# A transformer layer's down projection: seven products of half blocks in place of a direct product

## The chip, the cores and the metric
One core of a Trainium2 chip runs the whole kernel. The metric is the device time of one execution in microseconds (us). The kernel before takes 816.16 us, the median of three runs (816.03 to 816.21).

## The reference
One layer of a streaming encoder over 576 tokens (512 of a prompt, 64 of a sample), width 1024, all float32: normed input projection, two groups of attention heads, an output projection, cross-attention into a memory, and then the part that matters here:

```
hf = rms_norm(x, g_ffn)
x = x + (silu(hf @ w_gate) * (hf @ w_up)) @ w_down      # w_gate, w_up: 1024 x 2816, w_down: 2816 x 1024
y = rms_norm(x, g_final)
```

## The kernel before
Five engines run five hand-written queues, tied together by semaphores. Activations lie transposed in SBUF: 128 features on the partitions, 576 tokens in the free dimension, cut in two halves of 288 (`x_low`, `x_high`). Every float32 operand of a product is split into a rounded fp32r part (high) and a remainder (low), and one product is three matmuls: high by high, low by high, high by low (`product`, L499 to L501). ACT (ScalarE) writes the high parts of the weights, by a copy (L1123 for every ACT operation); POOL (GpSimd) subtracts to get the low parts of blocks that come as they are from memory; DVE (VectorE) does it for blocks that are sums.

**Gate and up projection.** Two of the 22 tiles of 128 hidden features are done early, directly. The other 20 (`NW`) are one step each. A step computes a gate tile and an up tile as a 2 x 2 block product with seven products in place of eight (`seven`, L1019), each of 4 k-tiles: 7 x 4 x 3 = 84 matmuls of 288 columns. For the weights of the next step DVE makes four sums of quarter blocks, 128x512 each (`weight_sums`, L2059), and four low parts (`op_rest`, L2081), and combines the products of the step at hand out of PSUM (L2116 to L2144); it multiplies the gate by the row `rstd` (L2146) and the gate by the up tile, into `hidf` (L2154). ACT makes seven high parts (`op_high`, L1452), a copy of one quarter into a PSUM bank (`quarter_copy`, L1471), a copy of the first product (`first_copy`, L1482) and the silu. POOL makes three low parts of 128x512 (`op_low`, L2390, L2395). PE's product 1 of a step needs the last combination of the step before (both use one PSUM bank), its product 6 needs the first combination of its own step. SP loads two blocks of 512 KB for each step as soon as POOL's low parts of the step two before are made (`pair_load`, L2551).

**Down projection.** The contraction over 22 hidden tiles is cut in three chunks (`DOWN_K` = 8, 8, 6 tiles). For each of eight output tiles and each chunk (24 blocks, `DOWN`) PE does k-tiles x 2 halves x 3 matmuls (`down_part`, L1048): 8 x 22 x 2 x 3 = 1056 matmuls. The output of one tile gathers in PSUM over all chunks. ACT makes the hidden tiles' high parts (`hid_high`, L1530), DVE their low parts (`hid_rest`, L2137, L2139), 22 of 128x576 each; ACT makes one high and POOL one low part of each weight block, 128x1024 or 128x768 (L2406 to L2409). When an output tile is done DVE multiplies it by `rstd`, adds it to `xb` (`residual`, L2188), and sums its squares; the last tile goes in two column parts (348 and 228) so that most of the final norm lies under the second part. Then come the column sums on PE (L1078), root, reciprocal, spreading on PE (L1087), and the outputs (L2218).

The names that the change's steps touch: `xb` (residual after the memory attention, eight tiles of 128x576), `rstd` (the third norm's reciprocal root, one row spread over all partitions), `tmp2`/`ut`/`gt`/`pp` (partial sums), `ss` and bank 6 (weight sums), `xs`/`xb` region, `hhi`/`hlo` (normed input, free once the last gate and up step has read them).

## Time and profile before

| what | value |
|---|---|
| median of three runs | 816.16 us |
| profiled execution, first to last instruction (span) | 814.9 us |
| around it: start and end of an execution that the span does not hold, median less span | 1.3 us |
| granted TensorE clock, mean of the span | 0.996 |
| PE busy | 798.7 us, 98% |
| DVE / ACT / POOL busy | 540.7 / 408.9 / 348.8 us |
| last gate and up step ends, down projection starts | 663.4 us |
| last matmul of the down projection ends | 806.2 us |

The profile gives no time of its own for the profiled execution beside its span. A busy PE here means that matmuls overlap: a matmul of 288 columns shows as 0.30 us, though the next starts 0.13 us after it. So PE's rate is read from the distance of starts, or from how many matmuls lie in a stretch. In a timeline, an instruction's duration holds the time in which it is held up by another engine after it was started; time in which it waits for a semaphore is shown as idle time before it, in brackets.

### The profile page before, as it was taken

The page shows a single profiled execution, that of the slowest core. Times are in us where ns is not written, and L with a number is a line of the kernel's source. Part 1 is how long each engine was busy: PE and PEld are TensorE (multiplying, and loading weights), DVE is VectorE, ACT ScalarE, POOL GpSimd, SP SyncE. Part 2 cuts the span into 40 slices and gives each one's busy share as a digit, 9 for nine tenths or more (in the row PEclk, how much of TensorE's full clock was granted, in tenths as well). Part 3 has the DMA queues.
Part 4 walks back from the last instruction along what each step waited for, and adds up shares of the span by engine and source line. Part 5 has one row for each costly group of instructions (what it writes and reads, how often), then busy time and mean ns, then how long its engine had stood idle before and what let it go on. Part 6 is the DMA issues. An engine that isn't in the chain of part 4 may idle for free.

```text
span 814.9 us, 15967 instructions
## 1 busy us (share of the span) xinstructions
PE 798.7 (98%) x5842; PEld 761.1 (93%) x5842; DVE 540.7 (66%) x970; ACT 408.9 (50%) x753; POOL 348.8 (43%) x258
## 2 busy tenths in 40 slices
...
DMA packets 26518, 75.90 MB, mean 93 GB/s; under 512 B 2896, under 2 KB 7448, under 8 KB 26328
## 3 DMA queue, kind: packets, MB, share of 16 engines
...
## 4 chain that ended last, share of the span: by engine, by line
PE 91%; DVE 3%; ACT 2%; issue 2%; DMA 1%; POOL 1%; SPq 0%; DVEq 0%; ACTq 0%
PE ps L499 28%; PE ps L500 27%; PE ps L501 27%; PE ps L658 2%; PE ps L676 2%; PE ps L517 1%; PE ps L928 1%; DMA wraw<-w_front 1%; POOL wlo L2244 1%; PE ps L525 1%; DVE xb L2218 1%; PE ps L641 1%; PE ps L913 1%; PE ps L640 1%; DVE probs L1774 0%
## 5 line engine op out<-in xcount | busy, mean ns | idle before, releaser
L499 PE MATMUL ps<-hhi,whi 128*128 128x288 f32 (+1 forms) x896 | 267.4, 298 | 6.7 <-DVE hlo L1613 5.8
L500 PE MATMUL ps<-hhi,wlo 128*128 128x288 f32 (+1 forms) x896 | 265.4, 296 | 0.0
L501 PE MATMUL ps<-hlo,whi 128*128 128x288 f32 x800 | 237.0, 296 | 0.0
L1123 ACT ACTIVATE whi<-wraw 128x1024 fp32r<-128x1024 f32 (+3 forms) x138 | 114.9, 838 | 136.2 <-PE ps L501 122.3
L499 PEld LDWEIGHTS ps<-hhi,whi 128*128 128x128 f32 x896 | 169.5, 189 | 8.5 <-DVE hlo L1613 5.7
L500 PEld LDWEIGHTS ps<-hhi,wlo 128*128 128x128 f32 x896 | 169.1, 189 | 0.2
L501 PEld LDWEIGHTS ps<-hlo,whi 128*128 128x128 f32 x800 | 150.9, 189 | 0.0
L2395 POOL TENSOR_TENSOR wlo<-wraw,whi 128x512 fp32r<-128x512 f32 x60 | 78.6, 1323 | 146.8 <-ACT whi L1123 146.8
L2244 POOL TENSOR_TENSOR wlo<-wraw,whi 128x256 fp32r<-128x256 f32 (+2 forms) x83 | 89.9, 1111 | 85.6 <-ACT whi L1123 85.4
L501 PE MATMUL ps<-hidlo,whi 128*128 128x288 f32 (+2 forms) x352 | 104.0, 296 | 0.0
L2409 POOL TENSOR_TENSOR wlo<-wraw,whi 128x1024 fp32r<-128x1024 f32 (+1 forms) x24 | 59.3, 2478 | 72.9 <-ACT whi L1123 72.9
L501 PE MATMUL ps<-tl,whi 128*128 128x288 f32 x240 | 71.4, 297 | 0.0
L500 PE MATMUL ps<-th,wlo 128*128 128x288 f32 x240 | 71.3, 297 | 0.0
L499 PE MATMUL ps<-th,whi 128*128 128x288 f32 x240 | 70.9, 295 | 0.0
L1123 ACT ACTIVATE whi<-ss 128x512 fp32r<-128x512 f32 x61 | 38.3, 631 | 63.8 <-PE ps L501 35.4
L501 PEld LDWEIGHTS ps<-hidlo,whi 128*128 128x128 f32 x352 | 66.2, 188 | 0.0
L2189 DVE TENSOR_TENSOR tmp<-ps,rstd 128x576 f32<-128x576 f32 (+2 forms) x9 | 6.2, 690 | 87.1 <-PE ps L501 87.1
L499 PE MATMUL ps<-hidhi,whi 128*128 128x288 f32 (+2 forms) x192 | 56.9, 297 | 0.0
L500 PE MATMUL ps<-hidhi,wlo 128*128 128x288 f32 (+2 forms) x192 | 56.9, 296 | 0.0
L1123 ACT ACTIVATE probs<-probs,small 128x128 f32<-128x128 f32 (+4 forms) x72 | 40.1, 557 | 32.8 <-DVE small L1774 32.4
L499 PEld LDWEIGHTS ps<-th,whi 128*128 128x128 f32 x240 | 45.2, 188 | 0.0
L500 PEld LDWEIGHTS ps<-th,wlo 128*128 128x128 f32 x240 | 45.2, 188 | 0.0
...
## 6 DMA issues: line engine op xcount, KB each, us to landing
...
```

What stands on the lines that cost most here:

```text
L499: nc.tensor.matmul(out, lh, rh, start=start, stop=False)
L500: nc.tensor.matmul(out, ll, rh, start=False, stop=False)
L501: return nc.tensor.matmul(out, lh, rl, start=False, stop=stop)
L517: mm = nc.tensor.matmul(ps[:, bank, at + tt:at + tt + 1], source[:, 128 * tt:128 * tt + 128], ones[:, 0:1], start=True, stop=True)
L525: mm = nc.tensor.transpose(out[:, at:at + n], col[0:n, tt:tt + 1].to_broadcast([n, 128]), ident[0:n, 0:n])
L640: nc.tensor.matmul(out, q1[r][:, q], k1[r][:, ks], start=True, stop=False)
L658: mm = nc.tensor.transpose(ps[:, 2 + s % 2, 128 * kb:128 * kb + 128], probs[:, P_AT[u] + 128 * kb:P_AT[u] + 128 * kb + 128], ident[:, :])
L676: mm = nc.tensor.matmul(ps[64 * e:64 * e + 64, 4, 128 * kb:512], va[:, g, kb, h + e, :], pt[e][:, 512 * kb:512 * kb + 512 - 128 * kb], sta ...
L1123: return nc.scalar.activation(out, src, func, **kw)
L2244: mm = g.tensor_tensor(wlo[:, b % 3, c], wraw[:, b % 2, c], f(whi[:, b % 3, c]), ALU.subtract)
L2395: g.tensor_tensor(w_operand(1, j), src, f(w_operand(0, j)), ALU.subtract).then_inc(g_lo, 1)
L2409: g.tensor_tensor(ffw(n, 1, 1, w)[:, 0, :], (wraw2, wraw)[n % 4 // 2][:, n % 2, 0:w], f(ffw(n, 0, 1, w)[:, 0, :]), ALU.subtract).then_inc( ...
```

## The change
The direct product of the down projection becomes twelve steps (`ND`): for each of the three chunks, four pairs of output tiles. A step is a 2 x 2 block product in seven products, as in the gate and up steps: two output tiles by two halves of the chunk's k-tiles (4, 4, 3: `D_KN`) by two halves of the tokens. The hidden tiles of a chunk need four sums or differences of quarters (`hidden_turn`), seven high parts (`hidden_high`, ACT) and seven low parts (`hidden_low`, POOL or DVE), of 128x1152 (chunks 0 and 1) or 128x864 (chunk 2). Each step needs four weight sums, seven high and seven low parts of 128x512 or 128x384 (`down_sums`, `down_high`, `down_low`, `down_rest`, `down_rest6`), and seven combinations of 128x288 on DVE. Products of different chunks no longer gather in PSUM: each step's results are added into a residual `xr` in SBUF, on POOL for the first ten steps (`add_low`, `add_rest`), on DVE for the last two (`final_add`). So that no multiplication by `rstd` is needed, the residual is first multiplied by `stdr` = 1/`rstd`, the third norm's root (`x_divided`, POOL, during gate and up steps 1 to 8), sent to DRAM and brought back to another place (2.36 MB each way); `sqacc` starts from EPS x D/128 x `stdr`^2, so that the final norm still has its epsilon. The last two steps are interleaved, and the final norm goes in two halves of 288 columns. `down_blocks` packs w_down chunk by chunk.

What stays is left out below, and so are the removed lines: `h_tile`, `hid_high`, `hid_rest`, `residual`, `squares`, the old `down_part` on PE and ACT, the old loops of POOL and SP, and the branches for the last gate and up step, which is now an ordinary one.

```diff
...
+        def quarter(tile, c, row, cols):
+    k0 = sum(DOWN_K[:c]) + D_KN[c] * row
+    return tile[:, k0:k0 + D_KN[c], cols]
...
+    def down(s, j):
+        c = s // 4
+        if j in W_POOL:
+            pe.wait_ge(g_lo, 4 + 3 * (NW + s) + W_POOL[j])
+        elif s == 0:
+            pe.wait_ge(w_vec, V_LAST + W_LOW[j])
+        elif j == 6:
+            after(pe, d_low6, s)
+        else:
+            after(pe, d_low, 3 * (s - 1) + j - 1)
+        if s % 4 == 0:
+            low_is_made(pe, c, j)
+        bank = W_BANK[j]
+        if s == 0 and j == 0:
+            pe.wait_ge(w_copy, 2 + 3 * (NW - 1))
+        elif s == 0 and j < 6:
+            pe.wait_ge(w_vec, V_LAST + W_FREE[j])
+        elif j == 0:
+            after(pe, d_first, s)
+        elif s == ND - 1 and j == 1:
+            after(pe, d_comb, comb_at(s - 1, "c11"))
+        elif s == ND - 1 and j == 4:
+            bank = 6
+        elif s == ND - 2 and j == 6:
+            bank = 7
+            after(pe, d_sum, 4 * (ND - 1))
+        elif j == 6:
+            after(pe, d_comb, comb_at(s, "c11"))
+        else:
+            after(pe, d_comb, comb_at(s - 1, COMB_FREES[j]))
+        if s == 0 and j == 6:
+            after(pe, d_comb, comb_at(0, "c11"))
+        for k in range(D_KN[c]):
+            mm = product(ps[:, bank, 0:HT], [down_operand(s, lo, j)[:, 128 * k:128 * k + 128] for lo in (0, 1)],
+                         [D_HI[c][j][:, k, :], D_LO[c][j][:, k, :]], k == 0, k == D_KN[c] - 1)
+        mm.then_inc(g_used, 1)
...
+    def last_columns(half):
+        for n0, source in enumerate((sqacc[:, 0:T], hidf[:, 14, :], hidf[:, 15, :])):
+            for n in range(LAST_N):
+                at = HT * half + LAST_W * n
+                mm = nc.tensor.matmul(ps[0:LAST_W, 2 + half, n:n + 1], source[:, at:at + LAST_W], ones[:, 0:1],
+                                      start=n0 == 0 and n == 0, stop=n0 == 2, skip_group_check=True)
+        mm.then_inc(n_col, 1)
...
+    for s in range(ND - 2):
+        for j in range(7):
+            down(s, j)
+    for s in (ND - 2, ND - 1):
+        for j in LOWS:
+            down(s, j)
+    down(ND - 2, 4)
+    down(ND - 2, 6)
+    after(pe, d_comb, comb_at(ND - 1, "c21"))
+    after(pe, e_acc, 6)
+    after(pe, e_sq, 4)
+    last_columns(0)
+    down(ND - 1, 4)
+    last_rows(0)
+    down(ND - 1, 6)
+    after(pe, e_acc, 8)
+    after(pe, e_sq, 6)
+    last_columns(1)
...
+    def hidden_high(c, j):
+        if j in T_ORDER:
+            turns_made(act, c, T_ORDER[j])
+        else:
+            act.wait_ge(w_vec, hid_at((7, 15, 21)[c]))
+        if c == 0 and j < 2:
+            after(act, x_saved, 16)
+        else:
+            act.wait_ge(g_used, D_PLACE[c][j])
+        activation(D_HI[c][j], D_SRC[c][j]).then_inc(h_hi[0], 1)
...
+    def down_high(s, j):
+        if s < ND - 1 or j not in HIGHS:
+            act.wait_ge(g_used, used_at(s - 1, j))
+        if j in (0, 1, 5):
+            down_loaded(act, s)
+            src = down_raw(s, *((0, 0) if j == 0 else (0, 1) if j == 1 else (1, 1)))
+        else:
+            after(act, d_sum, 4 * (s - 1) + {4: 1, 2: 2, 6: 3, 3: 4}[j])
+            src = down_sum(s, j)
+        activation(down_operand(s, 0, j), src).then_inc(g_hi, 1)
...
+    DOWN_EXTRA = {(2, 0): (1, 0), (2, 1): (1, 1), (4, 0): (1, 2), (4, 1): (1, 3), (4, 2): (1, 4), (4, 3): (1, 5), (4, 4): (1, 6),
+                  (5, 0): (2, 0), (5, 1): (2, 1), (7, 0): (2, 2), (7, 1): (2, 3), (7, 2): (2, 4), (7, 3): (2, 5), (8, 2): (2, 6)}
+    for s in range(1, ND):
+        down_first(s - 1)
+        for j in range(7):
+            down_high(s, j)
+            if (s, j) in DOWN_EXTRA:
+                hidden_high(*DOWN_EXTRA[s, j])
...
+    v.reciprocal(stdr[:, :], rstd[:, :]).then_inc(s_stdr, 1)
...
+    def down_sums(s):
+        a11, a12, a22 = down_raw(s, 0, 0), down_raw(s, 0, 1), down_raw(s, 1, 1)
+        a21 = ps[:, 7, 0:down_w(s)]
+        down_loaded(dve, s)
+        if s == 1:
+            dve.wait_ge(w_copy, 3 * NW)
+        else:
+            after(dve, d_a21, s - 1)
+            after(dve, d_low, 3 * (s - 1))
+        v.tensor_tensor(down_sum(s, 4), a21, a22, ALU.add).then_inc(d_sum[0], 1)
+        after(dve, d_sum, 4 * (s - 1) + 1)
+        v.tensor_tensor(down_sum(s, 2), down_sum(s, 4), a11, ALU.subtract).then_inc(d_sum[0], 1)
+        after(dve, d_sum, 4 * (s - 1) + 2)
+        if s > 2:
+            after(dve, d_low6, s - 2)
+        v.tensor_tensor(down_sum(s, 6), a12, down_sum(s, 2), ALU.subtract).then_inc(d_sum[0], 1)
+        v.tensor_tensor(down_sum(s, 3), a11, a21, ALU.subtract).then_inc(d_sum[0], 1)
...
+    def added(t, count, kept):
+        if t >= 1:
+            after(dve, d_add, min(3 * (t - 1) + count, 3 * (ND - 2)))
+        if t == ND - 1:
+            after(dve, e_x, kept)
+    def comb_c11(t):
+        after(dve, d_first, t + 1)
+        dve.wait_ge(g_used, used_at(t, 1))
+        added(t, 1, 1)
+        if t == 0:
+            dve.wait_ge(w_vec, V_LAST + V_N)
+        v.tensor_tensor(c11, ps[:, 1, 0:HT], pp[:, 0, :], ALU.add).then_inc(d_comb[0], 1)
...
+    def comb_up(t):
+        bank = 6 if t == ND - 1 else 4
+        dve.wait_ge(g_used, used_at(t, 4))
+        after(dve, d_comb, comb_at(t, "u3"))
+        added(t, 2, 5)
+        v.tensor_tensor(ut[:, x_high], ps[:, bank, 0:HT], partial(t, 2), ALU.add).then_inc(d_comb[0], 1)
+        added(t, 3, 6)
+        v.tensor_tensor(gt[:, x_high], ps[:, bank, 0:HT], partial(t, 1), ALU.add).then_inc(d_comb[0], 1)
...
+    def down_step(s):
+        t = s - 1
+        down_sums(s)
+        comb_c11(t)
+        comb_u2(t)
+        comb_u3(t)
+        down_low(s, 2)
+        down_low(s, 3)
+        if t < ND - 2:
+            comb_up(t)
+        down_low(s, 4)
+        comb_c21(t)
+        if t < ND - 2:
+            comb_c12(t)
...
+    hidden_low(0, 5)
+    hidden_low(0, 6)
+    VEC_EXTRA = {1: ((hidden_turn, 1, 4), (hidden_turn, 1, 3)), 2: ((hidden_turn, 1, 2), (hidden_turn, 1, 5)),
+                 3: ((hidden_low, 1, 0), (hidden_low, 1, 1)), 4: ((hidden_low, 1, 5), (hidden_low, 1, 6)),
+                 5: ((hidden_turn, 2, 4), (hidden_turn, 2, 3)), 6: ((hidden_turn, 2, 2), (hidden_turn, 2, 5)),
+                 7: ((hidden_low, 2, 3), (hidden_low, 2, 4), (hidden_low, 2, 5)), 8: ((hidden_low, 2, 6),)}
+    for s in range(1, ND):
+        down_step(s)
+        for work, c, j in VEC_EXTRA.get(s, ()):
+            work(c, j)
...
+    A, B = ND - 2, ND - 1
+    final_add(4, x_low, c11, A, "c11")
+    final_add(5, x_low, ut[:, x_low], A, "c21")
+    pair_acc(0, slice(0, T), 1)
+    pair_acc(1, slice(0, T), 2)
+    comb_c11(B)
+    comb_u2(B)
+    pair_acc(2, x_low, 3)
+    comb_u3(B)
+    comb_c21(B)
+    final_add(6, x_low, c11, B, "c11")
+    final_add(7, x_low, ut[:, x_low], B, "c21")
+    comb_up(A)
+    final_add(5, x_high, ut[:, x_high], A, "c22")
+    comb_c12(A)
+    final_add(4, x_high, gt[:, x_high], A, "c12")
             reciprocals(0)
+    comb_up(B)
+    final_add(7, x_high, ut[:, x_high], B, "c22")
+    pair_acc(2, x_high, 5)
+    outputs(0, True)
+    comb_c12(B)
+    final_add(6, x_high, gt[:, x_high], B, "c12")
+    outputs(0, False)
             reciprocals(1)
+    outputs(1, True)
+    outputs(1, False)
...
+    TURN_AT = {12: 4, 13: 3, 14: 2, 15: 5}
+    for n in range(NW + 1):
+        p = (n, None)
+        op_low(0, p)
+        op_low(1, p)
+        if 1 <= n <= KT:
+            x_divided(n - 1)
+        elif n == KT + 1:
+            square_start()
+        elif n in TURN_AT:
+            hidden_turn(TURN_AT[n])
+        elif n in (NW - 2, NW - 1):
+            hidden_low(0, n - NW + 2)
+        elif n == NW:
+            hidden_low(0, 2)
+            hidden_low(0, 3)
+        op_low(5, p)
+    hidden_low(0, 4)
+    def down_rest(s, j):
+        pool.wait_ge(g_hi, 4 + 7 * (NW + s) + j + 1)
+        src = down_raw(s, *((0, 0) if j == 0 else (0, 1) if j == 1 else (1, 1)))
+        g.tensor_tensor(down_operand(s, 1, j), src, f(down_operand(s, 0, j)), ALU.subtract).then_inc(g_lo, 1)
...
+    def add_low(t):
+        if t < 4:
+            after(pool, x_back[t], 16)
+        m = 2 * (t % 4)
+        after(pool, d_comb, comb_at(t, "c11"))
+        g.tensor_tensor(xr[:, m, x_low], xr[:, m, x_low], rstd[:, 0:HT], ALU.add).then_inc(d_add[0], 1)
+    def add_rest(t):
+        m = 2 * (t % 4)
+        after(pool, d_comb, comb_at(t, "c21"))
+        g.tensor_tensor(xr[:, m + 1, :], xr[:, m + 1, :], tmp2[:, 1, :], ALU.add).then_inc(d_add[0], 1)
+        after(pool, d_comb, comb_at(t, "c12"))
+        g.tensor_tensor(xr[:, m, x_high], xr[:, m, x_high], tmp2[:, 0, x_high], ALU.add).then_inc(d_add[0], 1)
+    REST_EXTRA = {4: ((1, 2), (1, 3)), 6: ((2, 0),), 7: ((2, 1),), 8: ((2, 2),)}
+    for s in range(1, ND):
+        t = s - 1
+        if t:
+            down_rest6(t)
+            add_rest(t - 1)
+        down_rest(s, 0)
+        down_rest(s, 1)
+        for c, j in REST_EXTRA.get(s, ()):
+            hidden_low(c, j)
+        if t < ND - 2:
+            add_low(t)
+        down_rest(s, 5)
+        if s == 4:
+            hidden_low(1, 4)
+    down_rest6(ND - 1)
...
+    for n in range(2, NW + ND):
+        sp.wait_ge(g_lo, 4 + 3 * (n - 1))
+        if n < NW:
+            pair_load(n)
+        else:
+            down_load(n - NW)
+        if n == KT + 2:
+            sp.wait_ge(x_scaled, KT)
+            sp.dma_start(x_dram, xb[:, :, :].rearrange("p a b -> p (a b)")).then_inc(x_saved[0], 16)
+        elif n == NW + 1:
+            sp.wait_ge(g_used, ff_used(G, 4))
+            after(sp, x_saved, 16)
+            for b in range(4):
+                sp.dma_start(xr[:, 2 * b:2 * b + 2, :].rearrange("p a b -> p (a b)"), x_dram[:, 2 * T * b:2 * T * b + 2 * T])\
...
```

`turns` gives quarter sources: 4 = high half of row 0 less low half, 3 = quarter(row 1, high) less quarter(row 0, high), 2 = quarter(row 1, high) less turn 4, 5 = quarter(row 1, low) less turn 2. `comb_u2`, `comb_u3`, `comb_c21`, `comb_c12` add one PSUM bank to one SBUF row of 288, as `comb_c11` does. `hidden_low` and `hidden_turn` on DVE and POOL are one tensor_tensor with both inputs in SBUF.

## Rows read from the trace of the kernel before

**Rows 1.** The page: busy time of each engine, its share, instructions.

```profile
PE 798.7 (98%) x5842; PEld 761.1 (93%) x5842; DVE 540.7 (66%) x970; ACT 408.9 (50%) x753; POOL 348.8 (43%) x258
```

**Rows 2.** Two stretches: gate and up, then down (last: clock, DMA share, GB/s).

```profile
620.00:645.00 25.00, 25.00 (x190) 25.00 (x190) 22.34 (x38) 13.70 (x25) 8.50 (x7) 1.00 0.33 112
720.00:745.00 25.00, 25.00 (x190) 25.00 (x189) 4.66 (x4) 5.49 (x6) 9.70 (x5) 1.00 0.27 80
```

**Rows 3.** Timeline of ACT: the quarter's copy in two neighbouring steps.

```profile
630.67 0.58 ACT L1123 ACTIVATE ps<-wraw 128x512 f32<-128x512 f32 x1
...
641.83 0.58 ACT L1123 ACTIVATE ps<-wraw 128x512 f32<-128x512 f32 x1
```

**Rows 4.** Timeline of DVE over one gate and up step: start, duration.

```profile
633.16 0.70 DVE L2071 TENSOR_TENSOR ps<-ps,wraw 128x512 f32<-128x512 f32 x1
...
634.62 1.47 DVE L2075 TENSOR_TENSOR ss<-wraw,ss 128x512 f32<-128x512 f32 x1
636.01 0.67 DVE L2076 TENSOR_TENSOR ss<-wraw,ps 128x512 f32<-128x512 f32 x1
636.61 0.44 DVE L2116 TENSOR_TENSOR tmp<-ps,pp 128x288 f32<-128x288 f32 x1
636.98 0.44 DVE L2120 TENSOR_TENSOR pp<-ps,pp 128x288 f32<-128x288 f32 x1
...
637.83 1.28 DVE L2081 TENSOR_TENSOR wlo<-ss,whi 128x512 fp32r<-128x512 f32 x2
...
641.30 0.46 DVE L2144 TENSOR_TENSOR tmp<-ps,tmp 128x288 f32<-128x288 f32 x1 [0.49 <-PE ps L501]
```

**Rows 5.** Timeline of POOL over the same step.

```profile
633.01 2.54 POOL L2395 TENSOR_TENSOR wlo<-wraw,whi 128x512 fp32r<-128x512 f32 x2 [2.55 <-ACT whi L1123]
640.32 1.29 POOL L2395 TENSOR_TENSOR wlo<-wraw,whi 128x512 fp32r<-128x512 f32 x1 [4.78 <-ACT whi L1123]
```

**Rows 6.** Timeline of DVE: wide operations ahead of the first step.

```profile
417.48 2.96 DVE L2041 TENSOR_TENSOR tf<-hf 128x1152 f32<-128x1152 f32 x1 [0.51 <-ACT hf L1123]
...
423.83 1.35 DVE L2041 TENSOR_TENSOR tf<-hf 128x1152 f32<-128x1152 f32 x1
425.10 3.57 DVE L2041 TENSOR_TENSOR tf<-hf,tf 128x1152 f32<-128x1152 f32 x1
```

**Rows 7.** Timeline of POOL over the same stretch, and later alone.

```profile
416.38 6.31 POOL L2372 TENSOR_TENSOR wlo<-wraw,whi 128x1024 fp32r<-128x1024 f32 x2 [6.45 <-DVE hlo L2021]
424.06 3.38 POOL L2372 TENSOR_TENSOR wlo<-wraw,whi 128x1024 fp32r<-128x1024 f32 x1 [1.37 <-ACT whi L1123]
...
672.49 2.40 POOL L2409 TENSOR_TENSOR wlo<-wraw,whi 128x1024 fp32r<-128x1024 f32 x1 [6.25 <-ACT whi L1123]
```

**Rows 8.** Narrow POOL operations by line: shortest, median and longest, ns.

```profile
L2347 POOL TENSOR_TENSOR xa<-xa,evt x16: 797/868/1722, 256.1 to 293.3; 128x288 f32<-128x288 f32 x16
L2339 POOL TENSOR_TENSOR sqacc<-sqacc,tmp x6: 1412/1424/1612, 173.6 to 279.4; 128x576 f32<-128x576 f32 x6
```

**Rows 9.** Timelines of POOL and DVE at the old down projection's start.

```profile
678.96 8.06 POOL L2409 TENSOR_TENSOR wlo<-wraw,whi 128x768 fp32r<-128x768 f32 x2 [4.07 <-ACT whi L1123]
...
682.79 0.74 DVE L2139 TENSOR_TENSOR hidlo<-hidf,hhi 128x576 fp32r<-128x576 f32 x1
```

**Rows 10.** Reciprocals by form: count, busy us, mean ns.

```profile
L1994 DVE RECIPROCAL small<-small 128x1 f32<-128x1 f32 x16 | 2.4, 151 | 0.0
L1878 DVE RECIPROCAL small<-small 128x10 f32<-128x10 f32 x8 | 1.6, 204 | 0.0
```

**Rows 11.** Timelines of DVE and the chain near the end of the first step.

```profile
452.01 0.45 DVE L2144 TENSOR_TENSOR tmp<-ps,tmp 128x288 f32<-128x288 f32 x1
...
452.69 0.21 PE ps L499
```

**Rows 12.** Timeline of the tail: last down matmul, then DVE to the last outputs.

```profile
805.95 0.27 PE L501 MATMUL ps<-hidlo,whi 128*128 128x228 f32 x1
...
809.36 2.18 DVE L2218 TENSOR_TENSOR xb<-xb,ps 128x456 f32<-128x456 f32 x3 [0.73 <-PE ps L1087]
```

More of the change, by code:

```diff
@@ L2193, in squares @@
[L2193 to L2205 removed]
+            step((NW, None))
@@ L2221, in _ @@
-            low, high = slice(0, LAST_AT[1]), slice(LAST_AT[1], T)
-            dve.wait_ge(d_half, 1)
-            residual(KT - 1, KT - 1, low, ps[:, 6, 0:low.stop], lambda a: a)
-            squares(KT - 1, low)
-            reciprocals(0)
-            outputs(0)
-            dve.wait_ge(g_used, 4 + 7 * NW + 3 * KT)
-            residual(KT - 1, KT, high, ps[:, 7, 0:T - high.start], lambda a: a)
+                at = LAST_S[half]
+                v.reciprocal(small[0:LAST_W, S_LRC + at:S_LRC + at + LAST_N], small[0:LAST_W, S_LSD + at:S_LSD + at + LAST_N])\
+                    .then_inc(n_rc, 1)
```

523 lines of the change are left out of this document (291 added, 232 removed).

## The prediction

> **What bounds the kernel now.** I read the page first, then stretches of equal length, then the timelines of DVE and POOL side by side. The page says PE is busy 98% of the span [rows 1], and the granted clock is 1.00 both in the gate and up steps and in the down projection [rows 2], so TensorE runs at its upper level (2.4 GHz) and work taken from PE is worth its time, as long as the other engines keep up. PE's rate: one gate and up step, 84 matmuls, lasts 641.83 - 630.67 = 11.16 us [rows 3], so 0.133 us for a matmul of 288 columns. The same stretches show the difference that decides this case. In a gate and up step DVE is busy 22.3 of 25 us, in the old down projection 4.7 of 25; POOL 8.5 and 9.7 [rows 2]. The old down projection is cheap for both, and the change turns it into steps like the others, with more work on both.
>
> **PE's part.** Removed: 1056 matmuls. Added: 7 products x 3 matmuls x (4 + 4 + 3) k-tiles x 4 pairs = 924. 132 fewer x 0.133 = **-17.5 us**. A step takes 11.16 us in chunks 0 and 1, 63 x 0.133 = 8.4 us in chunk 2; all twelve 122.9.
>
> **How DVE and POOL share.** Look at operations with two inputs in SBUF. POOL's two of 128x512 last from 633.01 to 635.55 [rows 5]. DVE's sum of two SBUF blocks (L2075) is started at 634.62 and shows 1.47 us, where its like (L2076, one input in PSUM) shows 0.67 [rows 4]: it ends at 636.09, 0.54 after POOL. The sum at 633.16, one input in PSUM, takes its usual 0.70 beside the same POOL operations. Wide ones show it better: of four DVE operations of 128x1152 (three stand there) one takes 1.35 alone, the others about 3, because three POOL operations of 2.4 alone lie between them, and two of these grow too [rows 6, 7]. From 416.38 to 428.67 is 12.3 us; three POOL operations (7.2) and four of DVE at 1.27 (the distance of 423.83 and 425.10) are 12.3. So the two engines take turns, with nothing gained by overlap. The Trainium skill ("SBUF — State Buffer", "Who interferes with whom") says that a VectorE instruction with two SBUF inputs contends with GpSimd instructions that read SBUF, as an exclusive lock held for a whole instruction. The trace agrees: 1.47 in place of 0.67. Without such a rule the sum would be that of rival (a).
>
> Exclusive durations, by distance of starts. DVE: 0.60 for 512 columns (636.01 to 636.61; the pair at 637.83 is 1.28 with its end), 1.27 for 1152, so 0.46 for 384 and 0.95 for 864; a combination of 288 out of PSUM 0.37, and not part of this [rows 4, 6]. POOL: 1.27 for 512 (two in 2.54), 2.4 for 1024, so about 2.7 for 1152, 2.05 for 864 and 0.97 for 384; 0.8 for 288, 1.4 for 576 [rows 5, 7, 8].
>
> **Load of a down step on this pair.** POOL: four low parts (5.1), `add_rest` (1.4 + 0.8), `add_low` (0.8) = 8.1. DVE: sum 6, low parts 2 and 3 = 1.8. Together 9.9 us of 11.16; with 384 columns 6.9 + 1.4 = 8.3 of 8.4. Into this go the hidden tiles of chunks 1 and 2: on DVE 8 x 1.27 + 8 x 0.95 = 17.8, on POOL 3 x 2.7 + 3 x 2.05 = 14.2, in all 32.0. They lie in POOL's loops 2 to 9 and DVE's work beside them: 6 x 9.9 + 2 x 8.3 + 32.0 = **108.0 us**. PE needs 7 x 11.16 + 8.4 = 86.5 for the same. The heaviest is loop 4: 9.9 + 2.5 + 8.1 = 20.5 us for 11.16 of PE. ACT has at most some 10.5 us in a step (seven high parts at 0.6, five hidden ones at some 1.1, two copies of 0.4 and 0.58 [rows 3]) and holds nobody.
>
> **The start.** From PE's start of down step 0, the pair first has the end of a hidden low part (1.5, an estimate: more than half of 2.7), POOL's third weight part (1.3), hidden low part 4 (2.7), step 1's three parts (3.8), `add_low` (0.8), and DVE's gate multiply, low part 6 and hidden multiply (2.0; 0.7 for 576 columns, between 0.60 and 1.27), hidden low parts 5 and 6 (2.5), sum 6 and two low parts (1.8): 16.4 us. The queue of DVE says the same: `hidden_low` 5 and 6 stand ahead of `down_sums` and `comb_c11` of step 0, for which PE's product 6 waits, due at 9.6. DVE has 0.5 + 0.7 + 0.6 + 0.4 (silu) + 0.8 + 2.5 + 2.8 + 0.4 = 8.7 us before it, plus turns with POOL's 1.3, 2.7 and 1.3, so about 14: PE stands some 4 us there.
>
> **Down, summed.** PE's product 1 of step 9 needs the last combination of step 8 (one bank). This is there 16.4 + 108.0 us after the start, less POOL's last two operations of loop 9, which may be later (1.8): 122.6. PE alone would be there at 8 x 11.16 + 8.4 + 1.2 = 98.9. Stalls: 23.7. In steps 9 to 11 PE is the bound again. Down: -17.5 + 23.7 = **+6.2**. Bounds of the stalls: 6% less, if fixed parts of operations overlap, and POOL's lag hides 2 more (-9); idle moments of the pair, when POOL waits for a combination and DVE for a turn, 1 us in each of eight loops (+8). I take the middle.
>
> **Gate and up steps.** The wide reciprocal (L2086's neighbour, 576 columns, once) has no row. 1 and 10 columns show 151 and 204 ns [rows 10], 5.9 ns a column, so 3.5 us; the lower end is the 0.7 of any other operation of that width. The Trainium skill ("VectorE: DVE Perf Modes", "First, the fixed hardware budget") says that the reciprocal runs its divide with a repeat count of 8; by its 0.96 GHz clock that would be 4.8 us, an estimate by the page that makes the sum 1.3 larger. The operation stands ahead of the first loop step, where DVE has no slack: it makes the last combination of the first step at 452.01 without idle time, and PE stalls for it just after [rows 11]. So **+3.5** (0.5 to 3.5). `x_divided`, 1.4 on POOL between its second and third part, lies in POOL's idle 4.8 us after 635.55 [rows 5], behind DVE's sum, and ends near 637.5, before DVE's low part 2 at 637.83 [rows 4]: 0. The four turns and two hidden low parts (2.7) reach into it by 1.0, but DVE has 0.49 idle each step [rows 4] and PE's product 1 comes 1.6 - 0.46 = 1.1 after: 0, up to +1. SP: the store of 2.36 MB behind the load of step 10 and the reload behind that of down step 1 delay a load in the same queue by some 7 us or more (112 GB/s at a DMA share of 0.33 [rows 2], so 340 at full share); loads are issued a whole step (11.16) ahead of the next: 0, up to +4. The extra adds of `xr` are in POOL's 8.1. The copies `down_first`, `down_a21` replace those of gate and up.
>
> **The tail.** After the last down matmul (806.2) the old kernel needs 8.7 us to the span's end [rows 12]: residual, square, sums, root, rows, 2.18 of outputs, then the last store. New: the combination (0.5) in front of the add, the square on 576 columns in place of 228 (+0.3), outputs of 1152 columns (1.3) and four of 288 (1.5) for 2.18 (+0.6), and `outputs(0)` of the first half before the last combination (+0.3): **+1.7** (0.5 to 3).
>
> **Sum.** +6.2 + 3.5 + 1.7 = +11.4. Span 814.9 + 11.4 = 826.3. The median stands 1.3 above the span of the profiled execution, so 816.2 + 11.4 = **827.6 us**.
>
> **Rivals.** (a) *PE stays the bound.* The turns fall into idle time as in the gate and up steps, where DVE was held up 0.8 us only in a step [rows 4]; a step of DVE without POOL is 0.74 + 0.74 + 0.6 + 0.6 + 3 x 0.6 + 7 x 0.39 = 7.2, with two wide ones 9.8, below 11.16, and the start has no stall (8.7 < 9.6). Then -17.5 + 3.5 + 1.7 = -12.3: 804. It decides where the pair's load of a step is under 11.16; against it are 12.4 and 20.5, and rows 6 and 7. For it: those rows are few. 16%. (b) *Partly hidden:* the pair costs only in loop 4 (9) and at the start (4), or half the stalls: -17.5 + 12 + 5.2 = 0 around 816 (811 to 820). 14%. (c) *POOL starves.* At the old start one POOL pair of 768 columns shows 8.06 us because DVE went through back to back until 683.5 [rows 9], 4.5 us without a turn. If DVE's wide pairs win like that where PE waits for POOL's weight parts, 1 to 2 us more in each of seven steps: 837. 12%. (d) mine, 821 to 833: 58%.
>
> **Range and chances.** 0.2% is 1.6 us, about what a measurement of this kernel can tell. (d) and (c) are slower, (a) faster; of (b) a third is within 0.2%, the rest split. Faster 0.21, same 0.05, slower 0.74. To leave out no more than 2 in 10 the range goes from 808 (of (a) only the milder end) to 836.
>
> **What would show it.** The down projection holds 924 matmuls of 288 columns; in the stretches of steps 1 to 8 PE busy falls below 90%, DVE's low parts (ss, whi) have a mean well above 0.68 and POOL's 512 ones above 1.29; PE waits for DVE's combinations in banks 1 to 5, most in step 4; the wide reciprocal shows 3 to 5 us. I am wrong if the step distance stays at 11.16 in steps 1 to 3, or if DVE and POOL overlap with two SBUF inputs each.

## The result and the profile after

The changed kernel takes **835.38 us** (median of four runs, 835.06 to 836.55) against 816.18 (816.03 to 816.42) before: ratio 1.0239, 95% interval 1.0225 to 1.0254, so 19.2 us slower. The profiled execution has a span of 832.9 us (814.9 before) and a mean granted clock of 0.983 (0.996). The forecast was 827.6, the range 808 to 836: the sign and the main mechanism held, the size was 7.8 us short.

The page of the changed kernel, busy time of each engine, answers to [rows 1]; under it PE and the granted clock in forty slices of the span (20.8 us each):

```profile
PE 794.2 (95%) x5733; PEld 753.0 (90%) x5733; DVE 650.9 (78%) x1131; ACT 444.3 (53%) x828; POOL 459.5 (55%) x336
...
PE   7999999999999999999998999999999979799984
...
PEclk9999999999999999999999999999999999899996
```

DVE has 110 us more, POOL 111. PE's busy time fell by 4.5 us only, though 132 matmuls of the down projection (17.5 us) went: above all because matmuls at the lower clock show longer (7.6 us, below) and the new kernel has more small ones. But for the 8 in the 22nd slice, where the wide reciprocal lies, the thin digits that are new lie in the down projection, from the 33rd slice on, and at the tail.

Five stretches of the down projection, cut where the last combination of a step is made (columns: length, then PE, weight load, DVE, ACT, POOL busy; clock, DMA share, GB/s); they answer to the second of [rows 2]:

```profile
684.00:696.00 12.00, 11.35 (x86) 11.15 (x85) 11.79 (x17) 7.23 (x12) 11.38 (x9) 1.00 0.27 89
696.00:708.00 12.00, 11.68 (x89) 11.48 (x88) 11.72 (x18) 5.34 (x10) 11.39 (x8) 1.00 0.27 89
708.00:724.00 16.00, 11.73 (x87) 11.29 (x86) 15.83 (x17) 11.78 (x17) 16.00 (x9) 0.97 0.21 67
724.00:739.00 15.00, 13.71 (x84) 13.50 (x84) 14.83 (x18) 5.53 (x10) 15.00 (x10) 0.80 0.22 70
739.00:750.00 11.00, 10.50 (x79) 10.53 (x80) 10.79 (x17) 4.02 (x8) 7.42 (x5) 1.00 0.28 97
```

Each stretch is one step, some 84 matmuls, 11.16 us of PE at its full rate. DVE shows as full in all of them, POOL in the first four; this holds the time in which one is held up by the other, so it is not all work. The 16 and 15 us are steps 3 and 4, where hidden parts of chunk 1 are made.

The lines of DVE and POOL between 680 and 780 us (count, busy us, mean ns):

```profile
L2362 DVE TENSOR_TENSOR wlo<-ss,whi 128x512 fp32r<-128x512 f32 x14 | 16.6, 1223 | 0.0
L2357 DVE TENSOR_TENSOR ss<-wraw,ss 128x512 f32<-128x512 f32 x7 | 7.6, 1091 | 0.2
L2362 DVE TENSOR_TENSOR wlo<-ps,whi 128x512 fp32r<-128x512 f32 x7 | 4.7, 677 | 0.0
...
L2734 POOL TENSOR_TENSOR wlo<-wraw,whi 128x512 fp32r<-128x512 f32 x19 | 29.2, 1549 | 1.7 <-ACT whi L1245 1.7
L2750 POOL TENSOR_TENSOR xr<-xr,tmp 128x576 f32<-128x576 f32 x7 | 15.7, 2249 | 0.0
L2752 POOL TENSOR_TENSOR xr<-xr,tmp 128x288 f32<-128x288 f32 x7 | 10.6, 1507 | 0.0
```

Low parts of one size, from the same line of the kernel: 1223 ns with two inputs in SBUF, 677 with one in PSUM. POOL's grew too (1.27 to 1.55; the residual's adds 1.4 to 2.25 and 0.8 to 1.5).

What PE waited for from 666 to 820 us (us in total, times, longest):

```profile
PE ps L618 <- DVE tmp L2414: 7.0, 5, 4.6
PE ps L618 <- POOL wlo L2734: 4.1, 4, 2.1
PE ps L618 <- DVE tmp L2287: 2.7, 1, 2.7
PE ps L1207 <- DVE tmp L2402: 2.5, 1, 2.5
PE ps L618 <- DVE rstd L2384: 0.9, 1, 0.9
```

L2414 is the last combination of a down step (`comb_c12`), L2287 that of a gate and up step. All waits for L2414 lie before 740 us, all for POOL's low parts of weights (L2734) behind that. The starts of L2414 serve as clock ticks below, X0 to X11: 684.74, 696.42, 708.10, 724.08, 738.92, 749.97, 762.83, 776.42, 787.02, 795.75, 813.32, 820.04. PE's first down matmul is at 666.27.

The longest stall, on the timelines of PE, POOL and DVE (start, duration):

```profile
724.67 0.58 PE L618 MATMUL ps<-tl,whi 128*128 128x288 f32 x1 [4.62 <-DVE tmp L2414]
725.05 0.44 PE L619 MATMUL ps<-tl,wlo 128*128 128x288 f32 x1
...
713.23 3.00 POOL L2734 TENSOR_TENSOR wlo<-wraw,whi 128x512 fp32r<-128x512 f32 x2
716.18 2.69 POOL L2710 TENSOR_TENSOR hlo<-olof,xqr 128x1152 fp32r<-128x1152 f32 x1
718.82 3.10 POOL L2710 TENSOR_TENSOR hidlo<-hidf,hidlo 128x1152 fp32r<-128x1152 f32 x1
...
716.87 5.59 DVE L2362 TENSOR_TENSOR wlo<-ss,whi 128x512 fp32r<-128x512 f32 x2
...
724.08 0.44 DVE L2414 TENSOR_TENSOR tmp<-ps,tmp 128x288 f32<-128x288 f32 x1
724.45 3.70 DVE L2339 TENSOR_TENSOR hhi<-hhif,hidlo 128x1152 fp32r<-128x1152 f32 x1
```

DVE's two low parts, 1.28 us alone, take 5.59: the first waits 2.0 us for the end of one hidden part of POOL, the second for the next one. Behind them in DVE's queue stand `comb_up`, `comb_c21` and `comb_c12` of step 3, and for the last one's bank PE waits.

**Where 19.2 us went**, by distance of starts in the two traces: gate and up steps +2.9 (T0, the first down matmul, 666.27 for 663.36); down projection +10.0 (152.9 us for 142.9 from the first to the end of the last down matmul); tail +5.1 (13.8 for 8.7); 0.9 around the span (2.2 for 1.3, each execution against its own span); and 0.3 by which the profiled execution (835.06) lies under the median. Of the 152.9, 122.9 are the 924 matmuls, 20.6 are PE's gaps, 7.6 are 75 matmuls about 0.24 us apart in place of 0.133, and the rest small matmuls.

### The profile page after: what moved, and what is told of

Same layout as the page of the kernel before. It is cut to its first block and busy times, and to the rows that moved or that the text cites. A ratio compares the mean times of both kernels' runs of the same rounds, so it can differ in the third digit from the quotient of the medians.

```text
span 832.9 us, 16155 instructions
## 1 busy us (share of the span) xinstructions
PE 794.2 (95%) x5733; PEld 753.0 (90%) x5733; DVE 650.9 (78%) x1131; ACT 444.3 (53%) x828; POOL 459.5 (55%) x336
## 5 line engine op out<-in xcount | busy, mean ns | idle before, releaser
L618 PE MATMUL ps<-hhi,whi 128*128 128x288 f32 x856 | 256.8, 300 | 11.2 <-DVE hlo L1762 5.6
L619 PE MATMUL ps<-hhi,wlo 128*128 128x288 f32 x856 | 254.0, 297 | 0.0
L1245 ACT ACTIVATE whi<-wraw 128x512 fp32r<-128x512 f32 (+3 forms) x150 | 112.4, 755 | 84.8 <-PE ps L620 70.1
L1245 ACT ACTIVATE whi<-ss 128x512 fp32r<-128x512 f32 (+1 forms) x97 | 59.6, 618 | 101.1 <-PE ps L620 38.8
L2230 DVE TENSOR_TENSOR wlo<-ss,whi 128x512 fp32r<-128x512 f32 x64 | 54.9, 884 | 0.0
L620 PE MATMUL ps<-hidlo,whi 128*128 128x288 f32 x176 | 53.5, 304 | 0.0
L2734 POOL TENSOR_TENSOR wlo<-wraw,whi 128x512 fp32r<-128x512 f32 (+1 forms) x33 | 47.7, 1460 | 4.5 <-ACT whi L1245 4.5
L618 PEld LDWEIGHTS ps<-th,whi 128*128 128x128 f32 x256 | 48.2, 188 | 1.1 <-issue 1.1
L619 PEld LDWEIGHTS ps<-th,wlo 128*128 128x128 f32 x256 | 48.2, 188 | 0.0
L620 PEld LDWEIGHTS ps<-tl,whi 128*128 128x128 f32 x240 | 45.1, 188 | 0.0
L777 PE MATMUL ps<-ident,probs 128*128 128x128 f32 x208 | 36.0, 273 | 0.5 <-DVE pt L1936 0.5
L620 PEld LDWEIGHTS ps<-hidlo,whi 128*128 128x128 f32 x176 | 34.8, 197 | 0.0
```

The lines of the kernel that those rows point to most:

```text
L618: nc.tensor.matmul(out, lh, rh, start=start, stop=False)
L619: nc.tensor.matmul(out, ll, rh, start=False, stop=False)
L620: return nc.tensor.matmul(out, lh, rl, start=False, stop=stop)
L777: mm = nc.tensor.transpose(ps[:, 2 + s % 2, 128 * kb:128 * kb + 128], probs[:, P_AT[u] + 128 * kb:P_AT[u] + 128 * kb + 128], ident[:, :])
L1245: return nc.scalar.activation(out, src, func, **kw)
L2230: v.tensor_tensor(w_operand(1, j), src, f(w_operand(0, j)), ALU.subtract).then_inc(w_vec, 1)
```

## The experiments

Eleven kernels, each run beside the kernel before on its chip. The column "against the changed kernel" is the difference to the kernel before less 19.2; T0 is the first down matmul. A run of two executions has an interval of 0.003 either way on its ratio (2.4 us), one of four 0.0017 to 0.0045 (1.4 to 3.6 us), and the changed kernel itself 0.0015. So a difference of two executions below some 2.7 us is not clear of noise: e1_spread, e3_warm, e8_loop4 and e10_start show no more by their totals than that nothing large was gained or lost, and what they tell is read from stretches of their traces.

| kernel | median us | ratio | against the changed kernel | span | T0 |
|---|---|---|---|---|---|
| changed | 835.38 | 1.0239 | | 832.9 | 666.27 |
| e1_spread | 833.85 | 1.0223 | -1.2 | 831.4 | 664.2 |
| e2_adds8 | 826.46 | 1.0132 | -8.6 | 824.7 | 666.67 |
| e3_warm | 837.12 | 1.0263 | +2.1 | 835.2 | 666.17 |
| e5_tail | 831.50 | 1.0200 | -3.1 | 828.4 | 666.07 |
| e6_low4 | 830.17 | 1.0178 | -4.9 | 828.6 | 667.24 |
| e7_low6 | 840.95 | 1.0316 | +6.4 | 839.4 | 666.56 |
| e8_loop4 | 836.42 | 1.0261 | +1.9 | 834.9 | 666.04 |
| e10_start | 836.28 | 1.0259 | +1.7 | 834.1 | 666.08 |
| e12_comb8 | 832.58 | 1.0207 | -2.6 | 830.6 | 666.32 |
| e13_psum | 827.23 | 1.0161 | -8.0 | 825.0 | 666.97 |
| e14_both | 829.67 | 1.0169 | -5.5 | 827.8 | 664.97 |

**e2_adds8: what POOL's adds into the residual cost.**

```diff
-g.tensor_tensor(xr[:, m, x_low], xr[:, m, x_low], rstd[:, 0:HT], ALU.add)
+g.tensor_tensor(xr[:, m, 0:8], xr[:, m, 0:8], rstd[:, 0:8], ALU.add)
```

(and the same for the two of `add_rest`: most of the residual's sum is left out.)

> POOL's adds into the residual (288 and 576 columns) are cut to 8 columns each with all waits kept, so y lacks most of the down projection of the first ten steps. This takes some 2.5 us from POOL's reads of SBUF in each loop and nothing from DVE's queue. Theory (the pair POOL and DVE share is overfull): DVE's wide operations lose their long waits (2.4 to 1.3 us), stalls of PE in steps 1 to 9 fall, time falls by 5 to 10 us. Rival (DVE's own queue is too long): within 1.5 us of the changed kernel.

Measured: -8.6, as the theory wanted (5 to 10) and the rival did not. X8 less T0 falls from 120.8 to 111.5 us. One stretch of its steps 1 and 2:

```profile
684.00:707.00 23.00, 23.00 (x168) 23.00 (x168) 22.52 (x35) 12.31 (x20) 15.63 (x15) 0.95 0.28 93
```

PE has no gap in it, POOL 7.4 us. So POOL's share of the pair's work costs time. It isn't the order between the two queues: from 666 to 800 us of the changed kernel DVE's combinations wait for the semaphore of a POOL add 0.5 us in all. But the sum of what is removed, some 2.4 us in each of nine loops (3.0 less 0.20 for each add of 8 columns), is 22: only a part of it came back, since PE needs its 11.16 in a full step whatever the pair does.

**e13_psum: the same turns from DVE's side.** Sum 6 and low parts 2 and 3 take an input from PSUM in place of SBUF, columns and order as before (they compute something else, and the copy of the next block waits for them).

```diff
-v.tensor_tensor(down_sum(s, 6), a12, down_sum(s, 2), ALU.subtract)
+v.tensor_tensor(down_sum(s, 6), a12, a21, ALU.subtract)
...
+src = ps[:, 7, 0:down_w(s)] if s < ND - 1 and j < 4 else down_sum(s, j)
-v.tensor_tensor(down_operand(s, 1, j), down_sum(s, j), f(down_operand(s, 0, j)), ALU.subtract)
+v.tensor_tensor(down_operand(s, 1, j), src, f(down_operand(s, 0, j)), ALU.subtract)
```

> Sum 6 and the low parts of operands 2 and 3 of each down step read the copy of the lower left block in PSUM in place of their SBUF sum, so that these three of DVE's operations have one input in SBUF; they compute something else, their number, columns and order are the same (ACT's copy of the next block waits for the two low parts). The prediction's pair load of a step falls from 9.9 to 8.1 us, DVE's own length stays. Theory A (DVE's queue plus its waits for POOL): sum 6 falls from a mean of 1.1 to 0.67 us and the low parts from above 0.8 to 0.65, so 0.7 to 1 us a step, some 5 us in all where the time is above PE's (4 to 7 us less than the changed kernel: 828 to 831). Theory B (sum of the pair): 1.8 x 8 = 14 less on the pair, so 10 to 13 us less, 822 to 825. Rival C (a lock only between the wide operations): below 2 us.

Measured: -8.0, between the two theories; one of its four executions took 833.69 us, the others 826.4 to 827.3, and with 3.6 us either way the total doesn't decide between them. X8 less T0 is 111.5 for 120.8. The same engine and columns, by line:

```profile
L2365 DVE TENSOR_TENSOR wlo<-ps,whi 128x512 fp32r<-128x512 f32 x21 | 13.7, 681 | 0.0
L2359 DVE TENSOR_TENSOR ss<-wraw,ps 128x512 f32<-128x512 f32 x7 | 4.8, 687 | 0.2
```

1223 and 1091 ns became 681 and 687: with one input in PSUM none of DVE's operations on the weights waits for POOL (its wide ones on the hidden tiles still do), and this is the cleanest proof of the mechanism. The largest gain is where the stall was: X2 to X3 takes 11.66 us in place of 15.98; X0 to X2 gains 0.5 (22.86 for 23.36), since PE sets the pace there.

**e12_comb8: DVE's own work, outside the turns.** The combinations of steps 0 to 10 touch 8 of 288 columns; most of the output of these steps is left out.

```diff
+def cut(ap, t):
+    return ap if t == ND - 1 else ap[:, 0:8]
...
-v.tensor_tensor(c11, ps[:, 1, 0:HT], pp[:, 0, :], ALU.add)
+v.tensor_tensor(cut(c11, t), cut(ps[:, 1, 0:HT], t), cut(pp[:, 0, :], t), ALU.add)
```

> The seven combinations of each of the down steps 0 to 10 touch 8 of 288 columns; instructions, order and waits stay, and the output loses most of the down projection. The combinations have one input in PSUM and no part in the turns between DVE and POOL, so the sum of the pair's operations is unchanged, while DVE's own queue gets shorter by 7 x about 0.3 = 2 us in a step. Theory A (refined after six runs: the step is set by DVE's queue in order, its own operations plus what it waits for POOL's): steps 1 to 8 get shorter by 1 to 2 us each where they are above 11.16, the time falls by 7 to 12 us against the changed kernel, to 823 to 828. Theory B (the prediction's: the sum of the two engines' exclusive operations sets the step): the same sum, so 0 to -2 us.

Measured: -2.6, where the queue theory wanted 7 to 12 and the pair's sum 0 to 2. Two stretches, as above:

```profile
696.00:708.00 12.00, 12.00 (x93) 12.00 (x92) 11.72 (x17) 5.94 (x12) 12.00 (x8) 1.00 0.27 89
...
724.00:739.00 15.00, 11.93 (x72) 11.61 (x72) 11.43 (x17) 4.66 (x9) 15.00 (x11) 0.80 0.21 71
```

DVE's work got shorter, its waits longer: low parts 1412 ns for 1223, POOL's `wlo<-ss,whi` 2059 for 1502. In steps 1 and 2 PE becomes the bound; in the heavy ones POOL is busy 15.00 of 15 while DVE stands idle 3.3 us, 1.9 for POOL's adds and 1.4 for PE, and X0 to X4 takes 52.1 us against 54.2 (X3 to X4 alone 18.3). There the pair's work is the limit, not the length of DVE's queue.

**e7_low6: the opposite trade.** The low part of operand 6 goes from POOL (1.27 us of a turn) to the end of DVE's loop (0.60).

```diff
-down_rest6(t)
...
+dve.wait_ge(g_hi, 4 + 7 * (NW + s) + 7)
+v.tensor_tensor(down_operand(s, 1, 6), down_sum(s, 6), f(down_operand(s, 0, 6)), ALU.subtract)
```

> The low part of operand 6 goes from POOL (1.27 us on the pair) to DVE (0.6). Theory (the pair's sum counts): 0.67 less in each of eight full loops, the time falls by 2 to 5 us although DVE has more to do. Rival (DVE's queue is the bound, whatever POOL does): 3 to 6 us slower, 0.6 in each loop.

Measured: +6.4, though the pair's sum falls by 0.67 us a step. Its steps 1 and 2, and the moved operation with the wide one behind it:

```profile
684.00:707.00 23.00, 22.04 (x155) 21.39 (x153) 22.62 (x28) 9.90 (x17) 17.94 (x11) 0.95 0.27 93
...
698.52 1.77 DVE L2431 TENSOR_TENSOR wlo<-ss,whi 128x512 fp32r<-128x512 f32 x1
700.21 1.96 DVE L2333 TENSOR_TENSOR olof<-hidf,hhif 128x1152 f32<-128x1152 f32 x1
```

POOL now has 5 us to spare, DVE none: the 0.60 became 1.77, because it too waits for an operation of POOL, and steps 1 and 2 take 13.1 us each for 11.7. PE waits five times, 10.1 us in all, for `comb_c11` (0.9 before). In light steps DVE's queue with its waits is the limit.

**e6_low4: the heavy loop.** POOL's three hidden low parts of chunk 1 (loop 4) become memsets, which read nothing (these low parts are left out).

```diff
+if c == 1:
+    g.memset(f(D_LO[c][j]), 0.0).then_inc(h_lopool[0], 1)
```

> The three low parts of hidden tiles that POOL makes in loop 4 (128x1152, one input pair in SBUF) become memsets of the same tiles: chunk 1's products lack these low parts. POOL still writes but reads nothing. Theory (20 us of work on the shared pair in loop 4): DVE's low parts beside them fall from 5.6 and 3.1 us to 1.3, the stalls of steps 4 and 5 (5.0 and 1.3 us) and the slow stretch behind them go, time falls by 7 to 9 us. Rival (DVE's own length, or ACT's seven hidden high parts in these steps): less than 2 us.

Measured: -4.9. Timeline of POOL, then of DVE:

```profile
717.17 1.06 POOL L2711 MEMSET hlo<- 128x1152 f32 x1
718.17 1.06 POOL L2711 MEMSET hidlo<- 128x1152 f32 x1
...
717.87 1.28 DVE L2362 TENSOR_TENSOR wlo<-ss,whi 128x512 fp32r<-128x512 f32 x2
```

The two low parts that showed 5.59 take 1.28, their time alone, beside a POOL that is busy writing. The stall of 4.8 is gone, and X0 to X4 takes 48.2 us for 54.2, the 6.0 that the theory is about. The total shows less because this execution's T0 came 1.0 later and its last step took 0.5 longer, neither of which the edit touches.

**e8_loop4: sharing loop 4 otherwise.** DVE makes hidden low parts 2, 3 and 4 of chunk 1, POOL 5 and 6.

```diff
-4: ((hidden_low, 1, 5), (hidden_low, 1, 6)),
+4: ((hidden_low, 1, 2), (hidden_low, 1, 3), (hidden_low, 1, 4)),
...
-REST_EXTRA = {4: ((1, 2), (1, 3)), 6:
+REST_EXTRA = {6:
```

> Chunk 1's five late hidden low parts are shared out otherwise: DVE makes those of products 2, 3, 4 behind step 4's queue, POOL those of 5 and 6 behind its last weight part. On the pair this is 1.4 us less, but above all no wide POOL operation lies beside DVE's two weight low parts of step 4. Theory: DVE's pair of low parts there falls from 5.6 and 3.1 us to 1.3, the stall of 4.8 us goes, that of step 5 grows by 1 to 2; time falls by 3 to 6 us. Rival (only the sum on the pair counts, wherever it lies): 1.4 us less.

Measured: +1.9. X2 to X3 falls from 15.98 to 11.68, X3 to X4 rises from 14.84 to 18.66: the turns moved one step on, with wide against wide:

```profile
720.59 3.78 POOL L2710 TENSOR_TENSOR hhi<-hhif,hidlo 128x1152 fp32r<-128x1152 f32 x1
...
721.77 3.82 DVE L2339 TENSOR_TENSOR hidlo<-hidf,hidlo 128x1152 fp32r<-128x1152 f32 x1
```

Neither theory had that; the two steps together take 30.3 us for 30.8. The +1.9 lies elsewhere, in the last step above all (see below).

**e10_start: the order at the start.** POOL's hidden low part 3 goes behind operand 5's, and DVE makes part 4 in place of POOL.

```diff
-    hidden_low(0, 3)
 op_low(5, p)
-hidden_low(0, 4)
+hidden_low(0, 3)
```

> At the change from gate and up to down: POOL makes hidden low part 3 behind its third weight part in place of ahead of it, DVE makes hidden low part 4 in place of POOL. Theory (the pair's order): DVE's two weight low parts fall from 5.6 us to 1.3, PE's stall of 2.8 us in step 0 product 1 goes; part of it comes back ahead of product 6, since the pair's sum falls by 1.4 only: 1 to 3 us less. Rival (the low part is then late for PE's products 3 and 4): no gain or 1 us more.

Measured: +1.7. The stall of 2.8 us at product 1 of step 0 becomes one of 0.3. But PE now stands 1.1 and 0.7 us ahead of products 4 and 5, whose hidden low parts DVE finishes just before (673.82 and 676.18 us), and what DVE took over also stands ahead of the combination for product 6:

```profile
681.83 0.37 PE L618 MATMUL ps<-th,whi 128*128 128x288 f32 x1 [3.72 <-DVE rstd L2384]
```

**e3_warm: is the lower clock a cost of its own?** Idle matmuls of 96 columns go before the last k-tile of five products, so that PE isn't idle ahead of the stalls. They spoil the running product (the relative error of y is 0.44), but leave the order and the number of the other operations as they are.

```diff
+for _ in range(WARM.get((s, j), 0) if k == D_KN[c] - 1 else 0):
+    nc.tensor.matmul(ps[:, bank, HT:HT + 96], ident[:, :], ident[:, 0:96], start=True, stop=True, ...)
```

> 40 idle matmuls (128x96, into free columns of the product's bank) are put ahead of the last k-tile of five products behind which PE would stand idle (steps 0, 4, 5 product 0, steps 6 and 8 product 6). Same result. Theory (each stall is followed by a stretch at the lower granted clock, 7.6 us in all): the slow matmuls after the long stalls of steps 0 and 4 go, time falls by 3 to 6 us though PE has more to do. Rival (only the waits count): no change or up to 2 us slower.

Measured: +2.1. The stretch behind the long stall, first of the changed kernel, then of this one:

```profile
725.00:730.00 5.00, 5.00 (x23) 5.00 (x23) 5.00 (x2) 1.44 (x2) 5.00 (x3) 0.51 0.65 210
```
```profile
725.00:730.00 5.00, 4.64 (x35) 4.67 (x36) 5.00 (x3) 2.56 (x4) 5.00 (x3) 1.00 0.65 210
```

PE stood idle 4.6 us ahead of the first, 1.0 ahead of the second, where the idle matmuls fill the rest. With 0.51 (the lower level, 1.2 GHz) matmuls come 0.24 us apart; with 1.00 (2.4 GHz) 0.133, and yet X3 to X4 takes 14.87 us for 14.84: PE is done sooner and waits for the same combinations. The lower clock in the middle of the down projection is an effect of the stalls and costs nothing beside them.

At the end it is otherwise. From X10 to X11 PE has 39 matmuls, and the last combination waits for them. No edit but those of e5_tail and e14_both touches this stretch. It takes 6.72 us at a granted clock of 0.75 in the changed kernel and 6.1 to 7.6 at 0.72 to 0.78 in e1, e2, e6, e7 and e12, but 7.75 at 0.56 in e10_start, 7.89 at 0.57 in e13_psum, 8.28 at 0.59 in e3_warm and 8.49 at 0.64 in e8_loop4. So some 1 to 1.8 us of the totals of e3_warm, e8_loop4 and e10_start lie there and say nothing about their edits.

**e1_spread: the reciprocal.** The root is spread from its column form by TensorE and copied by ACT, in place of DVE's reciprocal over 576 columns.

```diff
-v.reciprocal(stdr[:, :], rstd[:, :]).then_inc(s_stdr, 1)
...
+activation(stdr[:, 0:TP].rearrange("p (a b) -> p a b", a=4), ps[:, 4:8, HT:HT + 128])
```

> The third norm's root comes from spreading the deviations on PE and two ACT copies, in place of the 3.75 us reciprocal on DVE; same result. If the reciprocal costs what the trace of the changed kernel shows (PE idle 1.97 and 0.77 us after it, some slow matmuls), the time falls by 2 to 3 us and both idle moments go; five small transposes may give back up to 1. If DVE would be late there anyway, nothing changes (within 1 us).

Measured: T0 2.1 us earlier (1.3 in e14_both, which has the same edit), the span 1.5, the median 1.2. In kernels that are the same up to T0 it lies between 666.04 and 667.24, so the size is rough. In the changed kernel the reciprocal and PE's stall behind it are:

```profile
443.39 3.75 DVE L2253 RECIPROCAL stdr<-rstd 128x576 f32<-128x576 f32 x1
...
450.30 0.37 PE L618 MATMUL ps<-hhi,whi 128*128 128x288 f32 x1 [1.81 <-DVE tmp L2263]
```

**e5_tail: the end in another order.** The last two products, the column sums and DVE's `outputs(0)` change places, so that the last combination comes first; DVE's sums of squares go behind the first combinations of the last step (a part of the edit is shown).

```diff
-outputs(0, True)
 comb_c12(B)
 final_add(6, x_high, gt[:, x_high], B, "c12")
+outputs(0, True)
```

> Same work, the end in another order: PE does the last step's product 4 ahead of the first half's column sums, and sums the high half of sqacc before it waits for the last squares; DVE takes the last step's combinations before the sums of squares, and the last combination before the outputs of the first half. If the 13.9 us behind the last down matmul and the 32 us ahead of it (steps 9 to 11) come from this order (PE waits 2.7 us ahead of the first column sums, DVE is 0.9 late for the last combination, 18 small matmuls in one row of 2.9 us), the time falls by 3 to 5 us and nothing before step 9 moves. If they come from the amount of work alone, less than 1.

Measured: -3.1. Nothing before step 9 moved. ACT's square for the first column sums starts at 809.83 in place of 812.33, and PE stands 0.7 us ahead of them in place of 2.5.

**e14_both**: the two together, the fastest of the variants that compute the whole layer.

> The two edits of the earlier runs together, both with the computation unchanged: the root by spreading on TensorE in place of the wide reciprocal (-1.5 to -2.3 alone) and the reordered end (-3.2 to -3.9 alone). They lie at opposite ends of the down projection. If they add up: 829 to 831 us, ratio near 1.017. If the slack before the down projection is taken by DVE's queue, only the end's part is left: 831 to 832.

Measured: 829.67, -5.5; the two alone add to -4.3, and the intervals don't tell the two apart. It stays 13.7 us above the kernel before.

## Why the prediction was right, and where it was short

**Right: the turns of DVE and POOL.** It took from two places in the old trace that an operation of DVE with two SBUF inputs and one of POOL never overlap. e13_psum, e6_low4 and e2_adds8 show it from three sides: take the second SBUF input, the reading, or the length of POOL's away, and the waits go. The Trainium skill ("SBUF — State Buffer", "Who interferes with whom") states it as an exclusive lock; these runs agree (1223 against 681 ns). Rival (a), PE as the bound at 804 us, fell with the first stretch above: a step of 11.68 us for 11.16, though the forecast's other sign, PE busy below 90% in steps 1 to 8, holds in steps 3, 6 and 8 only (73, 84 and 84%). Rival (b), "the pair costs only in loop 4 and at the start", was close in place, but the start and loop 4 cost 4.7 and 4.8, and a dozen more gaps add 11.

**Right in number, only partly right in reason: the sum.** The last combination of step 8 was forecast 122.6 us after the start; X8 less T0 is 120.8. This is in part luck, since the terms miss both ways: X0 comes 18.5 us after T0 for a start of 16.4, and X0 to X8 takes 102.3 us for 108.0. Loop by loop the forecast's own terms are 12.4, 12.4, 20.5, 12.4, 13.9, 13.9, 13.2 and 9.3 (9.9 or 8.3 and the hidden parts that lie there); the distances of the ticks are 11.7, 11.7, 16.0, 14.8, 11.1, 12.9, 13.6 and 10.6. Nor does the path hold to its end: POOL stands idle 6.2 us ahead of the hidden part at 752.62, for a difference that DVE makes behind step 5, and from there to X8 PE waits for POOL's low parts of weights and not for a combination. The sum is not what sets each step: e7_low6 lowers it and is slower, e12_comb8 leaves it and is a little faster. By these two runs DVE's queue in order, with its waits for operations of POOL, sets the light steps (11.7 us) and the pair's own work the heavy ones; that one rule covers all steps isn't shown.

**Short: steps 9 to 11.** "In steps 9 to 11 PE is the bound again" is the step that failed. From X8 to the end of the last down matmul 32.1 us pass; by the forecast's terms it was to be 122.9 of PE less the 98.9 to step 8, 24.0. Of the 8.1 between them the trace shows 3.9 as waits: 2.7 before the first column sums, and 0.7, 0.3 and 0.3 elsewhere. The profile names `comb_up` of the last step but one (L2402) for the 2.7, but `last_columns(0)` waits for `comb_c21` of the last step, which is done at 811.6, and for ACT's square of its sums, which ends at 813.01; PE starts at 813.16. So it is the square, behind DVE's adds, as e5_tail confirms. Some 1.9 are small matmuls between the last products (the 18 of the first column sums and 3 of rows), and about 1.6 are fifteen matmuls 0.24 us apart. The forecast had nothing for any of these. With X8 1.8 us early this leaves the down projection 152.9 us long for a forecast 146.6. (As a difference it is +10.0 for +6.2, because the old projection took 142.9 where the forecast counted 140.4 for its matmuls.) The end, ACT's square and then PE's timeline:

```profile
812.33 0.68 ACT L1245 ACTIVATE hidf<-xr 128x576 f32<-128x576 f32 x1 [4.33 <-DVE xr L2453]
...
816.57 0.68 PE L1215 MATMUL ps<-ident,small 96*128 96x96 f32 x3
...
817.83 0.44 PE L618 MATMUL ps<-xqr,whi 128*128 128x288 f32 x1
818.07 0.44 PE L619 MATMUL ps<-xqr,wlo 128*128 128x288 f32 x1
...
821.85 0.94 PE L1207 MATMUL ps<-ones,sqacc 128*96 128x1 f32 x6 [2.71 <-ACT hidf L1245]
822.65 2.06 PE L1207 MATMUL ps<-ones,hidf 128*96 128x1 f32 x12
```

and a stretch of it, as above:

```profile
820.00:825.00 5.00, 2.86 (x18) 2.80 (x18) 2.71 (x8) 0.85 (x2) 0.00 (x0) 0.70 0.67 233
```

That the lower clock costs time here is read from the spread from X10 to X11 (6.1 to 8.5 us, given with e3_warm above); no run changes the clock alone.

**Short: the tail**, +5.1 for +1.7 (its bound was 3). On the right track was `outputs(0)` in front of the last combination (818.78 to 820.04 on DVE, 0.9 us late). Left out was the row of waits behind it: the add, ACT's squares, 18 column sums that end near 824.7 on a PE with a granted clock of 0.70 (from 820 to 825), root, reciprocal, rows. e5_tail gives 3.1 us of both parts back.

**About right: the reciprocal**, 3.75 us for the forecast 3.5 (6.5 ns a column for 5.9). Of the +2.9 on T0 (forecast +3.5) its own part is about 2: PE stood 1.97 and 0.77 us behind it, and e1_spread gave T0 2.1 back. A third stall, 0.84 us at 645.26, stays there without the reciprocal. It is the term put at "0, up to +1": POOL's hidden low part at 639.46 (3.13 us) lies beside DVE's two low parts, which take 4.31 in place of 1.28. The Trainium skill ("VectorE: DVE Perf Modes", "First, the fixed hardware budget") with its repeat of 8 had given an estimate of 4.8; the measured 3.75 decides.

**Right: the start**, a stall before product 6 for `comb_c11`, but it is 1.0 us, not 4; 2.8 came at product 1 already, whose bank waits for the last combination of the last gate and up step (L2287). DVE's two low parts ahead of it take 5.65 us (from 662.82) beside POOL's hidden low parts 2 and 3; the forecast had no term for that.

**Rival (c)**, 837, gives nearly the measured time for another reason: POOL does wait for DVE (1.55 for 1.27), yet what holds PE most is DVE's combination (7.0 us against 4.1 for POOL's low parts, all of the 7.0 before 740 us and all of the 4.1 behind it).

**Right at nothing:** the loads, the store and the reload of the residual. No wait of PE above leads to a transfer.
